# Two-block fp32 kernel on one core: both gate units of an FFN step issued ahead of the transposing DMA, memory and key pieces loaded alternately, one ScalarE copy moved

## What is computed

```python
# first block, DEPTH = 2, x is 256 x 1024, memory 256 x 1024
mem_kv = rms_norm(mem, mem_norm_g) @ mem_w_kv          # 1024 x 1024: keys, values
for i in range(2):
    x = x + 0.5 * swiglu(rms_norm(x, ffn1_norm_g[i]), ffn1_w_in[i], ffn1_w_out[i])
    proj = rms_norm(x, mix_norm_g[i]) @ (a_w_in if i == 0 else b_w_in)
    y_tok = mlstm_heads(...) if i == 0 else swa_heads(...)
    y_mem = memory_heads(...)                          # attention over the memory
    x = x + concat(y_tok, y_mem) @ w_out
    x = x + 0.5 * swiglu(rms_norm(x, ffn2_norm_g[i]), ffn2_w_in[i], ffn2_w_out[i])
# second block: hybrid_mixer, then one more swiglu of the same size, final rmsnorm
def swiglu(x, w_in, w_out):                            # 1024 -> 2 x 2816 -> 1024
    gate, up = split(x @ w_in, 2)
    return (silu(gate) * up) @ w_out
```

## Time and profile before

| | |
|---|---|
| median of 3 runs | 1565.52 us (1563.9 to 1565.69) |
| profiled execution: its own time, its span | 1567.18 us, 1565.5 us |
| PE busy | 1547.1 us, 99% of the span |
| DVE, ACT, POOL busy | 974.4, 809.8, 224.5 us |
| chain that ended last | PE 90%, DVE 4%, ACT 2%, issue 2%, POOL 1%, DMA 1% |

### The profile page before, as it was taken

The page is one execution under the profiler, slowest core; times in us unless marked ns, Lnnn a source line. Parts: engine busy times, 40 slices in busy tenths (PEclk is TensorE's granted clock), DMA queues, the critical chain, the costliest instruction groups (busy, mean ns, idle before and its releaser), DMA issues.

```text
span 1565.5 us, 20731 instructions
## 1 busy us (share of the span) xinstructions
PE 1547.1 (99%) x8283; PEld 1326.0 (85%) x8283; DVE 974.4 (62%) x1118; ACT 809.8 (52%) x998; POOL 224.5 (14%) x226
## 2 busy tenths in 40 slices
PE   8999999999999999999999999999999999999998
PEld 6888888988888888888978888899988899888886
DVE  6555566666655565545786555579898566665555
ACT  7544454555444454445557444466887434454444
POOL 1221100011111021110000211100562000011110
PEclk9999999999999999999999999999999999999999
DMA  7776666445767577665325776656554665557662
GB/s 255 230 221 208 186 186 210 138 144 177 230 206 216 170 212 224 201 194 176 108 82 162 235 208 204 209 165 216 168 190 142 223 186 184 186 175 228 208 210 92
DMA packets 264330, 296.13 MB, mean 189 GB/s; under 512 B 63260, under 2 KB 229560, under 8 KB 264248
## 3 DMA queue, kind: packets, MB, share of 16 engines
q1 hardware_dynamic: 263272, 293.70, 60.4%
q10 hardware_dynamic: 976, 1.31, 0.3%
HBM read 280.78 MB, written 1.09 MB: 180 GB/s over the span
## 4 chain that ended last, share of the span: by engine, by line
PE 90%; DVE 4%; ACT 2%; issue 2%; POOL 1%; DMA 1%; SPq 0%; DVEq 0%; POOLq 0%; ACTq 0%
PE ps L2106 24%; PE ps L2107 24%; PE ps L2108 24%; PE ps L2098 5%; PE ps L2100 4%; PE ps L2099 4%; PE ps L2241 1%; DMA scr<-in_mem_dram 1%; DVE w_lo L1241 0%; ACT w_hi L717 0%; DVE xg_lo L1271 0%; PE ps L2370 0%; POOL scr L660 0%; ACT xg_hi L737 0%; PE ps L2527 0%
## 5 line engine op out<-in xcount | busy, mean ns | idle before, releaser
L1241 DVE TENSOR_TENSOR w_lo<-w_raw,w_hi 128x2048 fp32r<-128x2048 f32 x255 | 589.3, 2313 | 371.2 <-ACT w_hi L717 371.0
L717 ACT ACTIVATE w_hi<-w_raw 128x2048 fp32r<-128x2048 f32 x255 | 487.4, 1913 | 388.1 <-PE ps L2108 333.3
L2106 PE MATMUL ps<-w_hi,xg_hi 128*128 128x512 f32 x1008 | 394.3, 391 | 0.6
L2108 PE MATMUL ps<-w_hi,xg_lo 128*128 128x512 f32 x1008 | 392.4, 389 | 0.0
L2107 PE MATMUL ps<-w_lo,xg_hi 128*128 128x512 f32 x1008 | 392.3, 389 | 0.0
L2106 PE MATMUL ps<-w_hi,y_hi 128*128 128x512 f32 x666 | 262.6, 394 | 0.0
L2108 PE MATMUL ps<-w_hi,y_lo 128*128 128x512 f32 x666 | 259.6, 390 | 0.0
L2107 PE MATMUL ps<-w_lo,y_hi 128*128 128x512 f32 x666 | 259.4, 390 | 0.0
L2098 PE MATMUL ps<-xg_hi,w_hi 128*128 128x256 f32 x800 | 229.4, 287 | 1.2 <-DVE w_lo L1248 0.5
L2099 PE MATMUL ps<-xg_lo,w_hi 128*128 128x256 f32 x800 | 226.3, 283 | 0.0
L2100 PE MATMUL ps<-xg_hi,w_lo 128*128 128x256 f32 x800 | 226.3, 283 | 0.0
(11 more groups left out here) (324 smaller groups left out, 1128.2 us busy)
## 6 DMA issues: line engine op xcount, KB each, us to landing
w_raw<-in_ffn_w_in_dram SPq DMA_DIRECT2D x176, 512.0 KB, 4.8
w_raw<-in_ffn_w_out_dram SPq DMA_DIRECT2D x88, 512.0 KB, 4.4
w_raw<-in_w_in_dram SPq DMA_DIRECT2D x82, 512.0 KB, 4.6
w_raw<-in_a_w_in_dram SPq DMA_DIRECT2D x28, 512.0 KB, 4.8
w_raw<-in_w_gate_dram SPq DMA_DIRECT2D x22, 512.0 KB, 4.0
w_raw<-in_w_up_dram SPq DMA_DIRECT2D x22, 512.0 KB, 5.0
w_raw<-in_w_down_dram SPq DMA_DIRECT2D x22, 512.0 KB, 4.1
w_raw<-in_w_ssd_proj_dram SPq DMA_DIRECT2D x16, 512.0 KB, 4.6
```

What stands on the lines that cost most here:

```text
L717: act.activation(w_hi[:, u % RING, :], w_raw[:, u % RING, :], ACT.Copy).then_inc(w_rounded, 1)
L1241: dve.tensor_tensor(w_lo[:, s, :], w_raw[:, s, :], w_hi[:, s, :].bitcast(F32), ALU.subtract).then_inc(w_split, 1)
L2106: pe.matmul(dst, xh, hi, start=start, stop=False, skip_group_check=True)
L2108: return pe.matmul(dst, xl, hi, start=False, stop=stop, skip_group_check=True)
```

## The change

Three edits that leave the arithmetic alone.

1. In `ffn`, SP issues both gate units of the next step ahead of `turn_back`; before, `turn_back` stood between them.
2. At the start the issue order of quarters and pieces is mixed, PE takes key tiles between the transposes of the quarters, ACT and DVE follow `KEY_ORDER`, `x` is loaded after the second value unit, and the two squares of the memory go ahead of `round_halves`.
3. In the first mixer `mem_turned` goes ahead of `high(3)` on ACT.

```diff
+        KEY_ORDER = ((0,), (1,), (2,), (3,), (), (4, 5), (), (6, 7))
...
                 gate_up(1, 0)
                 if f == 0:
                     small_inputs()
-                gate_up(0, 1)
+                for half in range(2):
+                    gate_up(half, 1)
                 for i in range(1, NI):
-                    gate_up(1, i)
                     load(u + 3 * i + 1, down_src(f, i - 1))
                     if i < NI - 1:
-                        gate_up(0, i + 1)
+                        for half in range(2):
+                            gate_up(half, i + 1)
                     turn_back(i - 1)
...
-                mem_quarter(sp, 2)
+                for j in range(1, 5):
+                    key_piece(sp, j)
                 mem_quarter(sp, 3)
-                for j in range(2, 8):
+                for j in range(5, 8):
                     key_piece(sp, j)
-                load(U["mem"] + 2, row_src(a["mem_w_kv"], 0, 512))
+                for j in range(2):
+                    load(U["mem"] + 2 + j, row_src(a["mem_w_kv"], 512 * j, 512))
                 sp.dma_start(x[:, :, :], a["x"][0].rearrange("(k p) d -> p k d", p=P)).then_inc(x_loaded, 16)
-                load(U["mem"] + 3, row_src(a["mem_w_kv"], 512, 512))
...
-                for k in (0, 1):
-                    columns(k)
-                for j in range(6):
+                for j, ks in enumerate(KEY_ORDER):
+                    for k in ks:
+                        columns(k)
                     round_piece(u + j // 4, j % 4, 4)
...
                 tanh(3)
+                mem_turned("A", pt_a, 4)
                 high(3)
-                mem_turned("A", pt_a, 4)
...
-            for q in (0, 1):
+            mem_quarter(act, 0)
+            key_piece(act, 0)
+            for q in (1, 2):
                 mem_quarter(act, q)
-            for j in (0, 1):
-                key_piece(act, j)
...
                 mem_turn_in(1)
-                pe.wait_ge(vec_done, vec.at("mem gain"))
+                key_tile(0)
                 mem_turn_in(2)
-                pe.wait_ge(xl_ready, 2)
+                key_tile(1)
+                key_tile(2)
                 mem_turn_in(3)
-                for k in range(8):
+                for k in range(3, 8):
                     key_tile(k)
```

More of the change, by code:

```diff
@@ L838, in columns @@
                     act.activation(y_hi[:, k], block_of(n, k), ACT.Identity, scale=col(gain, k)).then_inc(xh_ready, 1)
-                for k in (0, 1):
-                    columns(k)
-                for j in range(6):
+                for j, ks in enumerate(KEY_ORDER):
+                    for k in ks:
+                        columns(k)
                     round_piece(u + j // 4, j % 4, 4)
[L844 to L847, removed]
                 for tt in range(2):
                     square(n, tt)
+                round_halves(u + 2)
                 root(rn_y, rn_v, load=False)
@@ L858, in mem @@
                 act.activation(key_squares, key_rows, ACT.Square).then_inc(act_done, act_("M sq"))
+                round_(u + 4)
                 root(key_r, key_v, load=False)
-                round_(u + 4)
                 for half_ in range(2):
@@ L1406, in columns @@
                                              op0=ALU.mult, op1=ALU.subtract).then_inc(xl_ready, 1)
-                for k in (0, 1):
-                    columns(k)
-                for j in range(6):
+                for j, ks in enumerate(KEY_ORDER):
+                    for k in ks:
+                        columns(k)
                     split_piece(u + j // 4, j % 4, 4)
-                    columns(j + 2)
-                for j in (6, 7):
-                    split_piece(u + 1, j % 4, 4)
                 split_halves(u + 2)
```

## The result

| | before | after |
|---|---|---|
| median (lowest to highest) | 1564.85 us, 4 runs (1563.9 to 1565.69) | 1595.25 us, 4 runs (1592.87 to 1597.3) |
| ratio of the times, 95% interval | | 1.0183 (1.0171 to 1.0195) |
| profiled execution, its span | 1567.18, 1565.5 us | 1597.3, 1595.6 us |

The forecast was 1578.1 us with a range up to 1592. The sign was right, the size was not: +30.4 us instead of some +13. 1595.25 is close to what rival B gave, 1593.

A forecast was written before the change was run, and what follows sets the result against it. The prediction took PE, busy for 99% of the span, as the bound. 1567.18 + 15.5 (edit 1) - 1.5 (edit 2) - 1.4 (edit 3) = 1579.8 us, with the median 1.66 us lower: 1578.1 us, range 1569 to 1592.

The forecast's parts named there:

- rival B: The loop over five engines is longer than PE's step, nearly every step stalls 0.3 us: 1593 us, chance 0.17.
- What bounds the kernel, and the sign: PE is busy 99% of the span; in the FFNs edit 1 has no wait to remove, so the kernel gets slower.
- First step of an FFN: First transposition: join 3.21 us late, less 0.92 of cover, stalls PE 2.3 us; 11.5 us for five FFNs.
- rival D: PE's clock falls in the new stalls, some 2 us lost each time, seven times: 1592 us, chance 0.06.
- A: The forecast: first-step stalls of about 2 us per FFN, 5 to 6 in FFN 1, then recovery: 1571 to 1585, chance 0.64.
- I count 6.49 us from the issue of the load ahead of it: In the FFNs, the transposition waits for the load's data, so POOL's join begins 6.49 us after that load's issue.
- So an FFN works its delay off by some 0.4 to 0.5 us a step: After the first stall, a loop of 15.7 to 15.9 us against PE's 16.32 us step: no more stalls in steps 1 to 8.
- late landings: Slow transpositions in an FFN's first steps stall PE by what exceeds the margin: 1 us for all.
- FFN 1, 3 us for the rope: In steps 1 and 2 of FFN 1, 2.1 us of DVE rope work enters the loop, 1.6 us a step: 3 us.
- Edit 2, -1.5 us: At the start, PE warms up earlier on key tiles: -1.5 us, between 3.5 us gained and 0.5 us lost.
- Edit 3, -1.4 us: End of the first mixer: moving the four copies on ACT removes PE's wait: -1.4 us, between 0 and 1.4.
- Rival C: The transposition isn't held by the load, 0.4 us late inside the 0.92 of cover: 1562.6 or 1564.1 us, chance 0.13.

The follow-up runs named there:

- Experiment 11: Kernel before with the order of edit 1 for the first transposition of each FFN alone: 1584.26 us, ratio 1.0114.
- experiment 1: Kernel before with edit 1 alone, only the order of SP's issues in `ffn` changed: 1595.14 us against 1566.42, ratio 1.0179.
- Experiment 12: Kernel before with the order of edit 1 for the eight transpositions behind each FFN's first alone: 1577.02 us, ratio 1.006.
- Experiment 6: Kernel before with one of the second gate unit's two DMAs (512 KB) ahead of the transposition, the other behind it: 1575.45 us, ratio 1.0055.
- experiment 8: Edit 1 alone, with both pieces of FFN 1's rope work behind the split instead of one ahead of it: 1593.86 us, ratio 1.0173.
- Experiment 2: Changed kernel with the old order in `ffn`, so edits 2 and 3 without edit 1: 1565.79 us, ratio 0.9995.
- Experiment 4: Edits 2 and 3 without edit 1, with the two squares of the memory back behind the rounding: 1564.36 us, ratio 0.9986.
- experiment 3: Kernel before with edit 3 alone: 1565.32 us, ratio 0.9992.
- experiment 5: Kernel before, but SP waits for the second gate unit's free slot ahead of the transposition and loads that unit behind it: 1566.87 us, ratio 0.9996.
- experiment 10: Edit 1 alone, but ACT issues the transpositions from its own queue: 1600.12 us, ratio 1.021.

## Why the prediction was right or wrong

- **What bounds the kernel, and the sign**: right. Edit 1 has no wait to remove, and it sets the result.
- **First step of an FFN, 2.3 us each, 11.5 in all**: right in mechanism and near in size. Experiment 11 shows 12.2 us of waits. What it left out is the fall of PE's clock behind some of them, 3.2 us, which stood as rival D by itself at 0.06 though it is a rider on A and B alike.
- **"I count 6.49 us from the issue of the load ahead of it"**: this is the step that failed, in the loop. 6.49 was read where the transposition was issued 2.8 us behind the load and the unit before had landed. Right behind the load, the pair takes 6.74 us with an empty queue (first step), 6.94 us in the middle step shown, where the first gate unit is still in flight too, and the slowest 0.96 + 7.4 = 8.4. By the median landings that is 6.4, 6.7 and 7.1 us; no run tells the shorter head start and the unit in flight apart. "So an FFN works its delay off by some 0.4 to 0.5 us a step" therefore doesn't happen: the loop is 16.33 us and more against 16.32. Edit 1 as a whole cost 28.7 us (experiment 1) where the sum had 15.5. Experiment 12 prices the loop, +10.6 us for what I had put at 3 for the rope and 1 for late landings, with about half of it in FFN 1. Experiment 6 shows that the loop is the cause and not the delay as such, since with half of the data ahead the middle steps run at PE's pace.
- **FFN 1, 3 us for the rope**: the mechanism was right, and the size low: 4.4 us or more in the trace of experiment 8. The recovery of 0.5 us a step that I had set against it doesn't exist. The stretch from FFN 1 to FFN 2 grew by 10.8 us: two first waits (2.45 and 3.23), one fall of the clock, the rope and the loop.
- **Edit 2, -1.5 us**: the gain is there at the start, the loss in "the squares ahead of `round_halves` cost nothing". I asked what covers PE and not whom SP waits for. Experiments 2 and 4 differ in that alone, 1565.79 and 1564.36. With the squares back, edits 2 and 3 together give 2.1 of the 2.9 us that I had for them.
- **Edit 3, -1.4 us**: the wait went as forecast; 1.6 us in the trace of experiment 3, 1.1 in the median.
- **Rival B** was right in kind: it named the margin of 0.4 us as the point from which it decides, and 7.2 us as the value at which the loop loses. It had a chance of 0.17 on the ground that "the row has 6.49 with the same amount ahead". The amount was the same, but the head start of 2.8 us wasn't, and neither was the queue ahead of it.
- **Rival C** (a transposition that isn't held) is excluded by experiments 5, 6 and 1 together: 2.7, 4.7 and 5.9 us with nothing, 512 KB and 1 MB right ahead of it.

Open is why a separate queue doesn't shorten the landing. The runs show only that the transposition lands about 1 us behind the load that was in flight ahead of it, whatever queue it stands in. Open too is why PE's clock fell behind some waits and not behind others of the same length. The loop-bound kernels scatter more (the changed one from 1592.87 to 1597.3, experiment 1 from 1593.27 to 1598.87), so differences of 1 or 2 us between them aren't read.

## What to carry to other kernels

Before a DMA is moved behind a load, count the bytes asked for ahead of it and the time since they were asked for, and not only its place in the program: here the wait could be moved at no cost and the data couldn't. Around a busy engine, add up every loop that passes through the other engines and compare it with that engine's step, link by link; a margin of a few tenths of a microsecond with one uncertain link is no margin, and beyond it each step pays. An edit on one engine is hidden only if nobody waits on its semaphore whose own queue is on the path; ask that of the DMA queue first.

## What of the hardware was not expected

- A small transposing DMA lands 2.7 us after its issue by itself, 4.7 us right behind 512 KB and 5.9 us right behind 1 MB (medians of 50). With 1 MB right behind it, still 2.7. On another engine's queue behind 1 MB it takes 6.7 us (median of the 32 that stand so), counted from the load's issue the same 7.1 us as on the load's own queue. In each case it lands 0.7 to 1.1 us (medians) behind the last part of the load ahead of it.
- PE's granted clock went to 0.50 after waits as short as 2.02 and 2.20 us and stayed at 1.00 after others from 2.03 us (experiment 1) up to 2.59 us (experiment 8). One such fall of eight or nine matmuls costs 1.6 to 1.8 us where PE sets the pace; experiments 8 and 10 each had one that lasted about twice as long.
